# The beginning of a two-block transformer kernel: order of the first loads, size of the transfers, place of the memory values, and identity products on TensorE

## The reference, cut to what matters

```python
mkv = jnp.matmul(mem, w_mem_kv).astype(jnp.float32).reshape(B, N_MEM, 2, MEM_HEADS, HEAD_DIM)
mk, mv = mkv[:, :, 0], mkv[:, :, 1]
h = layer_norm(x, ln_in_g, ln_in_b)
for i in range(DEPTH):                    # four layers: a, b, c, a
    proj = jnp.matmul(h, w_in_a[j])       # gate (1280 columns) and memory queries (256)
    branch = fourier_mix(h)               # in a layer of kind a
    mem_out = memory_attention(qm, mk, mv)
    y = jnp.concatenate([branch, mem_out], axis=-1) * jax.nn.silu(gate)
    h = layer_norm(DEEPNORM_ALPHA * h + jnp.matmul(y, w_out[i]), ln_g[i], ln_b[i])
```

## Time and profile before

| | |
|---|---|
| three runs, median (lowest to highest) | 1345.26 us (1341.03 to 1345.51) |
| the profiled execution's own time | 1344.37 us |
| its span | 1342.6 us |
| TensorE busy, share of the span | 1270.0 us, 95% |
| VectorE busy | 864.9 us, 64% |
| ScalarE busy | 701.7 us, 52% |
| mean granted clock of TensorE | 0.988 |
| read from memory | 195.20 MB, 146 GB/s over the span |

### The profile page before, as it was taken

The page is one execution under the profiler, slowest core; times in us unless marked ns, Lnnn a source line. Parts: engine busy times, 40 slices in busy tenths (PEclk is TensorE's granted clock), DMA queues, the critical chain, the costliest instruction groups (busy, mean ns, idle before and its releaser), DMA issues.

```text
span 1342.6 us, 19912 instructions
## 1 busy us (share of the span) xinstructions
PE 1270.0 (95%) x7972; PEld 1110.9 (83%) x7972; DVE 864.9 (64%) x1518; ACT 701.7 (52%) x1015; POOL 2.4 (0%) x8
## 2 busy tenths in 40 slices
PE   5999999999999999998998998999999997999997
PEld 5997777778888787887887986989898986989895
DVE  5646996586564756548456886665546887665645
ACT  3624477453457566565525675544443676544442
POOL 0000000000000000000000000000000000000000
PEclk8999999999999999999998998999999999999998
DMA  9325432445543335233333443456564543456560
GB/s 299 116 78 188 157 111 79 157 137 200 181 155 121 126 118 166 85 126 102 126 119 113 154 138 100 151 185 211 167 216 118 157 144 112 148 180 219 163 223 40
DMA packets 146913, 197.53 MB, mean 147 GB/s; under 512 B 4716, under 2 KB 102278, under 8 KB 146694
## 3 DMA queue, kind: packets, MB, share of 16 engines
q1 hardware_dynamic: 146694, 196.22, 45.5%
q0 software_dynamic: 128, 0.04, 0.0%
HBM read 195.20 MB, written 1.05 MB: 146 GB/s over the span
## 4 chain that ended last, share of the span: by engine, by line
PE 77%; DVE 13%; ACT 5%; issue 4%; DMA 1%; SPq 0%; DVEq 0%; ACTq 0%
PE bank L461 21%; PE bank L462 21%; PE bank L463 21%; PE bank L547 4%; DVE w_lo L2079 4%; DVE stat L2099 2%; PE bank L749 2%; PE bank L1036 1%; PE bank L1073 1%; ACT w_hi L1542 1%; DVE arena L2093 1%; PE bank L660 1%; PE bank L898 1%; DMA arena<-in_mem 1%; DVE stat L2096 1%
## 5 line engine op out<-in xcount | busy, mean ns | idle before, releaser
L2079 DVE TENSOR_TENSOR w_lo<-w_raw,w_hi 128x2048 fp32r<-128x2048 f32 (+5 forms) x190 | 413.3, 2183 | 131.6 <-ACT w_hi L1542 129.3
L1542 ACT ACTIVATE w_hi<-w_raw 128x2048 fp32r<-128x2048 f32 (+5 forms) x190 | 346.1, 1828 | 284.8 <-PE bank L463 274.2
L461 PE MATMUL bank<-h_hi,w_hi 128*128 128x256 f32 x976 | 279.7, 287 | 5.3 <-DVE w_lo L2079 2.1
L462 PE MATMUL bank<-h_lo,w_hi 128*128 128x256 f32 x976 | 276.1, 283 | 0.0
L463 PE MATMUL bank<-h_hi,w_lo 128*128 128x256 f32 x976 | 276.0, 283 | 0.0
L461 PE MATMUL bank<-w_hi,r_hi 128*128 128x512 f32 (+3 forms) x536 | 208.4, 389 | 5.0 <-DVE r_lo L2753 4.2
L462 PE MATMUL bank<-w_lo,r_hi 128*128 128x512 f32 (+3 forms) x536 | 205.0, 382 | 0.0
L463 PE MATMUL bank<-w_hi,r_lo 128*128 128x512 f32 (+3 forms) x536 | 204.9, 382 | 0.0
L461 PEld LDWEIGHTS bank<-h_hi,w_hi 128*128 128x128 f32 x976 | 187.0, 192 | 12.1 <-issue 7.6
L462 PEld LDWEIGHTS bank<-h_lo,w_hi 128*128 128x128 f32 x976 | 187.1, 192 | 0.6
L463 PEld LDWEIGHTS bank<-h_hi,w_lo 128*128 128x128 f32 x976 | 187.1, 192 | 0.0
(11 more groups left out here) (283 smaller groups left out, 1370.5 us busy)
## 6 DMA issues: line engine op xcount, KB each, us to landing
w_raw<-in_mlp_w SPq DMA_DIRECT2D x64, 1024.0 KB, 5.4
w_raw<-in_w_out SPq DMA_DIRECT2D x24, 1024.0 KB, 5.1
w_raw<-in_w_in_c SPq DMA_DIRECT2D x48, 512.0 KB, 4.6
w_raw<-in_w_in_c SPq DMA_DIRECT2D x18, 1024.0 KB, 5.1
w_raw<-in_w_in_a SPq DMA_DIRECT2D x12, 1024.0 KB, 5.9
w_raw<-in_w_in_b SPq DMA_DIRECT2D x12, 1024.0 KB, 5.2
w_raw<-in_w_in SPq DMA_DIRECT2D x8, 1024.0 KB, 5.2
w_raw<-in_w_out SPq DMA_DIRECT2D x8, 512.0 KB, 3.8
```

Of the source, the lines that this page charges most:

```text
L461: nc.tensor.matmul(o, lhs[0], rhs[0], start=start, stop=False)
L462: nc.tensor.matmul(o, lhs[0], rhs[1], start=False, stop=False)
L1542: nc.scalar.activation(w_hi[:, u % SPLIT_SLOTS, 0:kts * n], w_raw[:, u % RAW_SLOTS, 0:kts * n], ACT.Copy).then_inc(w_rounded.sem, w_rounde ...
L2079: v.tensor_tensor(w_lo[:, s, 0:m], w_raw[:, u % RAW_SLOTS, 0:m], w_hi[:, s, 0:m].bitcast(F32), ALU.subtract)\
```

## The change

It touches the beginning alone. The memory rows are loaded ahead of unit 0; x comes in 4 transfers of 64 rows; the tables come in two parts, the later one (from `axial_cos` on, which the second layer reads first) after unit 6, with a semaphore of its own on which VectorE waits in the layer of kind b. TensorE makes 14 products of the identity with itself before the memory rows are there, and 6 products of the identity with 512 columns of the memory rows after these are turned; nothing reads their results. The values' product moves ahead of turning x. ScalarE rounds unit 0 after the high parts of the memory rows and unit 2 between two halves of x, and evacuates keys and values ahead of the tiles of x. VectorE cuts unit 1 between the statistics and the norm of the second block.

```diff
@@ TensorE
             pe.wait_ge(ident_loaded, 16)
+            for _ in range(14):
+                nc.tensor.matmul(bank[3][:, 0:P], ident, ident, start=True, stop=True)
             pe.wait_ge(mem_loaded, 16)
...
                 .then_inc(product_done.sem, product_done.next(("cols", "a")))
+            for _ in range(6):
+                nc.tensor.matmul(bank[3][:, :], ident, mem_in[:, 0, 0:512], start=True, stop=True)
...
             feature_major(("mem", "k"), 4, rows_of(A["w_mem_kv"], 0, KT, 0, MEM_W), rT)
-            hidden_from_rows("in", 0)
             u, w = unit(rows_of(A["w_mem_kv"], 0, KT, MEM_W, MEM_W))
...
             unit_done[u] = ("mem", "v")
+            hidden_from_rows("in", 0)
@@ SP
             sp.dma_start(const[:, 0:P], A["const"][:, 0:P]).then_inc(ident_loaded, 16)
+            sp.dma_start(mem_in, A["mem"][0].rearrange("(b p) d -> p b d", p=P)).then_inc(mem_loaded, 16)
             load_unit(0)
-            sp.dma_start(mem_in, A["mem"][0].rearrange("(b p) d -> p b d", p=P)).then_inc(mem_loaded, 16)
             xv = A["x"][0].rearrange("(c b a) d -> a b c d", a=4, b=4)
             for a in range(4):
-                for b in range(4):
-                    p0 = (a % 2) * 64 + b * 16
-                    sp.dma_start(x_in[p0:p0 + 16, a // 2, :], xv[a, b]).then_inc(x_loaded, 16)
+                p0 = (a % 2) * 64
+                sp.dma_start(x_in[p0:p0 + 64, a // 2, :], xv[a]).then_inc(x_loaded, 16)
             load_unit(1)
             load_unit(2)
             sp.dma_start(const_once, A["const"][:, n_kept:]).then_inc(consts_loaded, 16)
-            sp.dma_start(const[:, P:], A["const"][:, P:n_kept]).then_inc(consts_loaded, 16)
+            late = CONST_AT["axial_cos"][0]
+            sp.dma_start(const[:, P:late], A["const"][:, P:late]).then_inc(consts_loaded, 16)
...
                 load_unit(u)
+                if u == 2 * RAW_SLOTS:
+                    sp.dma_start(const[:, late:], A["const"][:, late:n_kept]).then_inc(tables_loaded, 16)
@@ ScalarE
-            round_unit(0)
             for j in range(4):
                 act.wait_ge(product_done.sem, product_done.at(("mem", "t", j)))
                 nc.scalar.activation(flat2(r_hi[:, 2 * j:2 * j + 2, :]), bank[4 + j][:, :], ACT.Copy).then_inc(split_hi.sem, split_hi.next(("mem", j)))
+            round_unit(0)
+            evac(("cols", "a"), col_a[:], bank[0][:, 0:N_COL_A], ahead=0)
             round_unit(1)
-            evac(("cols", "a"), col_a[:], bank[0][:, 0:N_COL_A])
-            act.wait_ge(x_loaded, 256)
+            act.wait_ge(x_loaded, 64)
             for b, n in BY_SCALAR:
+                if b == 1:
+                    round_unit(2)
                 act.wait_ge(row_stats.sem, row_stats.at(("in", b)))
...
+            evac(("mem", "k"), flat2(mkT[:, :, :]), bank[4][:, :], ahead=0)
+            evac(("mem", "v"), flat2(mv[:, :, :]), bank[5][:, :], ahead=0)
             hidden_hi("in", "a0", split_t, tiles_read)
...
             nc.scalar.activation(ident_r[:], ident, ACT.Copy).then_inc(tables_rounded.sem, tables_rounded.next(0))
-            evac(("mem", "k"), flat2(mkT[:, :, :]), bank[4][:, :])
-            evac(("mem", "v"), flat2(mv[:, :, :]), bank[5][:, :])
+            round_weights(("a0", "qm"), 1)
@@ VectorE
                     if j in js:
-                        product((L, "zt", j))
+                        product((L, "zt", j), 1 if L == "in" else SPLIT_SLOTS - 1)
...
             weights(("mem", "k"), 0)
-            dve.wait_ge(x_loaded, 256)
+            dve.wait_ge(x_loaded, 64)
             for b in range(NB):
                 for n in range(2):
                     link(v.bn_stats(S_(128 + 12 * b + 6 * n, 6), x_in[:, b, n * 512:(n + 1) * 512]))
+                if b == 1:
+                    weights(("mem", "v"), 0)
                 row_norm("in", b)
             normal_half("in", x_in[:, 1, 0:512])
-            weights(("mem", "v"), 0)
+            weights(("a0", "qm"), 0)
...
                 elif kind == "b":
                     dve.wait_ge(rows_b_loaded, 16 * ROW_B_DMAS)
+                    dve.wait_ge(tables_loaded, 16)
```

More of the change, by code:

```diff
@@ L262, in build @@
         consts_loaded = ctx.enter_context(nc.semaphore("consts_loaded"))
+        tables_loaded = ctx.enter_context(nc.semaphore("tables_loaded"))
         x_loaded = ctx.enter_context(nc.semaphore("x_loaded"))
```

## The result

The changed kernel takes 1358.34 us in the median of four runs (1356.83 to 1359.85); the kernel before took 1343.14 beside it. The ratio is 1.0111, 95% interval 1.0095 to 1.0128: 15 us slower, clear of noise and outside the range that was given (1340.2 to 1351.1). The profiled execution has a span of 1356.8 against 1342.6.

What follows compares the result with a forecast made beforehand. TensorE, busy 95% of the span, bounds the kernel; VectorE's early chain sets the gate product at 40.84. The head's gain is spent on moving the values, loads 0: sum 0.0, forecast 1344.4, range 1340.2 to 1351.1.

Steps and rivals of the forecast that it cites:

- the price of x's transfers: Loads: x in four transfers lands at 14.1 at 205 GB/s or 11.6 at 411, needed at 15.3; taken as 0.
- rival 1: New x transfers: only four engines serve them, x lands at 19.2, values start late; 1348.4 or 1351.1 us; chance 0.28.
- Rival 4: Before the gate product: open waits of 2.1 and 2.7 lower the clock; 1.6 to 4.4, 1346.0 to 1348.8; chance 0.08.
- The identity products: Fourteen TensorE products from 2.7 until 8.0, bounds 7.2 and 8.6; the memory rows' turning then starts, against 11.08.
- the rise of the clock: During the identity products: full TensorE clock 3.0 to 6.1 us after their start at 2.7, taken at 7.2.
- the wide products: Six TensorE products between turned memory rows and keys, 5.2 to 5.5 us in all; cost nothing, cover 0.1 to 0.3.
- The move of the values: Values' 5.8 us on TensorE now ahead of turning x; first tile at 29.8, spending what was gained in front.
- Late tables, look-aheads and the added wait: Late table part behind unit 6, look-ahead naming the same units, VectorE's wait long satisfied: 0, or one 0.4 us issue.
- The first tile's sum: VectorE's first x tile at T+21.8 = 29.8, with T = 8.0 the start of turning the memory rows.
- the forecast's own case: Whole beginning: sum 0.0, bounds -0.8 to +1.1, forecast 1344.4; chance 0.45.
- Rival 2: Values' product hidden after all: VectorE alone sets the first tile at 27.3, gain 2.5, 1341.9; chance 0.15.
- Rival 3: Clock stays at 0.50 past the memory rows' turning; wide products take 10.3 us, keys end at 32.6; 1354.2; chance 0.04.

Runs made afterwards that it cites:

- x_near_rows_4: The kernel after, x still in four transfers to 64 partitions, each reading 64 neighbouring rows instead of four blocks of 16; 1345.16 us, ratio 1.0003.
- x_one_transfer: The kernel after with x in one transfer to 128 partitions, two rows each, neighbouring rows to neighbouring partitions; one run, 1345.7 us.
- before_x4: The kernel before with one part of the change alone, x in four transfers of 64 rows; 1352.62 us, ratio 1.0062.
- x4_alone: The kernel after with one wait added: SP issues unit 1 only when x has landed; 1355.16 us, ratio 1.0077.

## Why the prediction was wrong

**The step that failed** is the price of x's transfers, in the part on loads: "at 205 GB/s, as x moves now, it takes 5.1 us after unit 0 (from about 9), lands at 14.1; at 411, 11.6. Both in time; I take 0." Both ends were taken from rows of transfers whose outer dimension is 16 or 128. The new one has 4, x landed at 26.88, and by `x_near_rows_4` the loss goes with it. "No row shows a transfer of four separate blocks of rows" was seen, and the case was put into rival 1 with 0.28 instead of into the bounds of the term.

**Rival 1** had the mechanism: four engines, VectorE idle before its statistics, unit 1 late, the clock down in the values. Its size was off. Its landing of 19.2 is what x does alone (20.02). It let unit 1's part wait behind x for 3.0 more, and that is what happened (2.6); but it left x's rate at 103 GB/s, where x moved at 50 while units 1 and 2 moved on the other engines, and x took 6.9 us longer (26.88). Its start of the values, 26.7, was 34.17; its 2.7 for the slow clock was 1.9. With 1351.1 as the upper end the range ended 7 us short. The Trainium skill, DMA: Bandwidth & Descriptors, "Why a DMA increments its semaphore by 16 and not by 1", on how many engines a DMA uses, gave four for this shape; the share of 0.25 agrees, and with it 0.28 was too low a chance.

**Rival 4** came true as well, in the gate product: 0.51 from 55.4 to 58.9, 1.5 us (it had 1.6 to 4.4), after the open waits that the forecast had named. It was set beside rival 1 as another case, where it adds to it. Nor does it need a late x: behind the same wait of 1.95 the clock was down in `x_near_rows_4` and not in `x_one_transfer`, from 43 to 44 us in both:

```profile
43.00:44.00 1.00, 1.00 (x6) 1.00 (x6) 1.00 (x2) 0.55 (x1) 0.00 (x0) 0.50 1.02 364
...
43.00:44.00 1.00, 1.00 (x11) 1.00 (x10) 1.00 (x3) 0.82 (x1) 0.00 (x0) 1.00 1.02 364
```

So an open wait of 2 us can cost 1.5 us more or nothing, and no run here shows what decides.

**Right, point by point.** The identity products end and the memory rows are turned from 8.28 (forecast 8.0), the rise of the clock being in time. The memory rows land 5.6 us after their issue at 1.18, at 6.8 (7.0). Unit 0's low part 12.90 (13.1), the keys 15.34 (15.5), the wide products done by then and never in the way. From the first tile to the gate product 54.27 - 43.23 = 11.04, as worked out. The move of the values takes back the head's gain: with x on time the first tile is at 29.94 (29.8) and the gate product at 40.98 (40.8), and the time that of before. Late tables, look-aheads and the added wait cost nothing that these runs show.

**Slips of the working**, without effect on the range. No row shows the 3.0 us that the rise of the clock is given as its lower bound: the first burst ran at the low pace for all of its 3.4 us. The first tile's sum, 20.5 + 1.1 + 0.3, is T+21.9, and the upper end of the forecast's own case, 0.6 + 0.3, is +0.9 and not +1.1.

**Rival 2** (the values hidden after all) did not happen: VectorE waits 2.58 for TensorE before the first tile even with x in one transfer. **Rival 3** did not: the wide products run at full clock, 5.35 us for twelve records.

**Where the gain of the head goes.** 2.85 us at unit 0's low part. With 16 transfers the wait for x until 15.2 to 15.8 takes some of it, the values ahead of the turn the rest; behind the turn, and with unit 3 rounded in time, 3.0 us are kept.

## What to carry to other kernels

When transfers are put together to save issues, look at the outer dimension of both sides: four blocks of 16 rows in one transfer used 4 of 16 engines; that saved 5 us of issue time and cost 8.4 us in the kernel before and nearly all of the 15 in the kernel after. A long wait of one load spreads: what is issued behind it on the same engines is late in part of its pieces, and that part counts. And before a product is moved ahead of a chain in order to fill TensorE, ask what it covered where it stood.

## What the runs showed of the hardware that was not expected

- A load on few engines is slowed by loads on the others. On its four engines x moved at 50 GB/s while units 1 and 2 moved on the twelve others, and at 86 to 100 without them; units 1 and 2 moved at 131 GB/s then. On the four engines themselves unit 1's part waited behind x. What the engines wait for in common is open.
- x's rate differed with the form of its transfers, with all sixteen engines busy: 148 GB/s with two rows to each of 16 neighbouring partitions, 175 to 207 with one row to each of 16, whether the source rows are neighbours or 64 KB apart, 219 to 250 with 64 partitions, 392 with 128. The distance of the source rows does not decide; the target and the count of transfers changed together. Why is open.
- SP's issue of the third transfer behind x (`const_once`) ended when x had landed: at 26.96 in the kernel after (x at 26.88), 26.35 in `before_x4` (26.27), 16.99 with 8 transfers (17.15), 14.98 with 16 (15.17). With x already there, in `x4_alone`, it took 1.19 us. Nothing on the chain hung on it here.
